# Four raw retention gates of each layer computed in the first attention heads; the first queries' waits and three weight splits placed differently

## The reference, cut to what matters

```python
(rq, rk, rv, rg, cq, ckv, kr, gq, gk, gv, gates) = jnp.split(p, split_at, axis=-1)   # p = h @ w_in
# retention, 4 heads of 128 (q, k) and 256 (v): decayed scores, then the readout
y = rms_norm(y).reshape(B, T, RET_W)
return (jax.nn.silu(g.astype(jnp.float32)) * y).astype(g.dtype)                      # g = rg
# latent attention, 8 heads; grouped-query attention, 8 query heads on 2 key heads
p = softmax(q @ k.T * scale); y = p @ v
# merge
z = sigmoid(gates0) * (y_ret @ w_ret_o) + sigmoid(gates1) * (y_mla @ w_mla_o) + sigmoid(gates2) * (y_gqa @ w_gqa_o)
x = x + mod2 * (z @ w_out)
```

## Time and profile before

| what | value |
|---|---|
| median of three runs | 3587.95 us (3586.75 to 3588.75) |
| profiled execution | 3589.15 us, span in the trace 3587.4 us |
| mean granted TensorE clock | 0.958 of full |
| PE busy / PEld / DVE / ACT / POOL | 3253.7 / 2750.4 / 1517.0 / 1256.1 / 397.5 us |
| chain that ended last | PE 45%, issue 7%, DVE 5%, ACT 2%, DMA 1%, POOL 1% of the span |
| DMA | 309.76 MB, mean 86 GB/s |

### The profile page before, as it was taken

The page is one execution under the profiler, slowest core; times in us unless marked ns, Lnnn a source line. Parts: engine busy times, 40 slices in busy tenths (PEclk is TensorE's granted clock), DMA queues, the critical chain, the costliest instruction groups (busy, mean ns, idle before and its releaser), DMA issues.

```text
span 3587.4 us, 50087 instructions
## 1 busy us (share of the span) xinstructions
PE 3253.7 (91%) x18776; PEld 2750.4 (77%) x18776; DVE 1517.0 (42%) x2025; ACT 1256.1 (35%) x1769; POOL 397.5 (11%) x304
## 2 busy tenths in 40 slices
PE   6799997999898988899999978998799898889998
PEld 5688876888787777788888857787677776768886
DVE  4555423445335433422222355553455455443334
ACT  3344432445323332221211233443255444432222
POOL 0011100111102101010100101110011101011001
PEclk9899998999999999999999988998899899989999
DMA  4122141111331133123132422222121232232222
GB/s 178 56 71 75 69 127 37 59 53 59 107 107 54 60 117 128 49 83 128 59 132 79 138 103 74 69 85 77 54 71 64 71 116 69 85 105 94 99 94 99
DMA packets 98094, 309.76 MB, mean 86 GB/s; under 512 B 10832, under 2 KB 20176, under 8 KB 98000
## 3 DMA queue, kind: packets, MB, share of 16 engines
q1 hardware_dynamic: 55872, 202.40, 16.8%
q10 hardware_dynamic: 42128, 106.07, 8.8%
HBM read 281.17 MB, written 27.26 MB: 86 GB/s over the span
## 4 chain that ended last, share of the span: by engine, by line
PE 45%; issue 7%; DVE 5%; ACT 2%; DMA 1%; POOL 1%; ACTq 0%; DVEq 0%; POOLq 0%
PE ps L1334 43%; PE ps L1437 1%; DVE mx L875 1%; PE ps L1415 1%; POOL ptl L1316 1%; ACT wh L399 1%; DVE tmp L854 1%; DVE wl L844 0%; DVE ptl L893 0%; DMA mraw<-in_wmod 0%; DVE tmp L914 0%; ACT pth L452 0%; ACT side L475 0%; PE ps L1451 0%; DVE hl L1053 0%
## 5 line engine op out<-in xcount | busy, mean ns | idle before, releaser
L1334 PE MATMUL ps<-hh,wh 128*128 128x512 f32 x2768 | 826.9, 359 | 84.6 <-DVE wl L844 33.2
L1334 PE MATMUL ps<-hl,wh 128*128 128x512 f32 x2768 | 815.2, 355 | 0.0
L1334 PE MATMUL ps<-hh,wl 128*128 128x512 f32 x2768 | 815.1, 355 | 0.0
L844 DVE TENSOR_TENSOR wl<-raw,wh 128x1024 fp32r<-128x1024 f32 x364 | 484.7, 1332 | 683.8 <-ACT wh L399 657.1
L1334 PEld LDWEIGHTS ps<-hh,wh 128*128 128x128 f32 x2768 | 456.7, 192 | 173.8 <-issue 46.8
L1334 PEld LDWEIGHTS ps<-hl,wh 128*128 128x128 f32 x2768 | 456.5, 192 | 73.9
L1334 PEld LDWEIGHTS ps<-hh,wl 128*128 128x128 f32 x2768 | 454.9, 191 | 75.4
L399 ACT ACTIVATE wh<-raw 128x1024 fp32r<-128x1024 f32 x364 | 382.4, 1051 | 246.4 <-PE ps L1334 204.9
L1334 PE MATMUL ps<-yh,wh 128*128 128x512 f32 (+1 forms) x1296 | 410.7, 371 | 37.9 <-DVE yl L1185 17.1
L1334 PE MATMUL ps<-yl,wh 128*128 128x512 f32 (+1 forms) x1296 | 398.0, 362 | 0.0
L1334 PE MATMUL ps<-yh,wl 128*128 128x512 f32 (+1 forms) x1296 | 397.6, 361 | 0.0
(11 more groups left out here) (185 smaller groups left out, 3471.7 us busy)
## 6 DMA issues: line engine op xcount, KB each, us to landing
raw<-in_stream SPq DMA_DIRECT2D x364, 512.0 KB, 3.3
mraw<-in_wmod ACTq DMA_DIRECT2D x40, 512.0 KB, 3.3
prob<-in_wmod ACTq DMA_DIRECT2D x40, 512.0 KB, 3.3
gspill<-prob ACTq DMA_DIRECT2D x32, 384.0 KB, 2.3
tmp<-gspill ACTq DMA_DIRECT2D x24, 384.0 KB, 3.1
early<-in_wmod SPq DMA_DIRECT2D x16, 512.0 KB, 15.1
vraw<-gspill ACTq DMA_DIRECT2D x16, 384.0 KB, 3.6
dec<-in_dec ACTq DMA_DIRECT2D x8, 768.0 KB, 4.3
```

Of the source, the lines that this page charges most:

```text
L844: dve.tensor_tensor(wl[:, s, :], raw[:, s, :], wh[:, s, :].bitcast(F32), ALU.subtract).then_inc(sem("w_lo"), 1)
L1334: ins = pe.matmul(out, lhs[w], rhs[x](cols), start=start and n == 0, stop=stop and n == 2)
```

## The change

**Plan.** Of each retention head's two gates the second (column tile 2h+1) is no longer projected in `ret`. The four of a layer are projected in the first heads, two in `mla_first` (heads 0 and 1) and two in `gqa_first` (heads 2 and 3), with 768 columns in layer 0 and 512 in layer 1. The weight chunks move with them in the stream. The results are spilled to a new DRAM tensor `gheld` and read back in `ret`.

**First heads.** The held gates use the slots 1 and 0 in this order, between the first query's projection and the rest of the first head. TensorE's wait ahead of the first query is now for the query ranks alone (`mla_first`) or for the last `vl` (`gqa_first`); in `mla_first` a wait for all ranks stands before the key's projection.

**Splits.** In `mla_in` split 5 stands before the second square root and reciprocal. In `gqa_in` split 3 stands after the first square root on ACT and after the first reciprocal on DVE. In `ret` a head has three chunks: split 4 stands after the one gate's Silu on ACT, is left out in the last head, and split 5 is gone.

**`ret`.** Two heads a loop turn (`half_turn`). ACT issues the DMA of the held gate after the key's rotation, takes its Silu in place after split 4, and then goes on to the `pth` copies. TensorE waits for the two slots after the first two scores instead of before them.

```diff
+HELD = {"chunk": 2, "free0": 1, "free1": 1, "g_out": 2}
-        phase("mla_first", layer, 0, {}, total(head, head, *raws, attention(nq, first=1)), nt=nt)
+        phase("mla_first", layer, 0, {}, total(head, head, HELD, *raws, attention(nq, first=1)), nt=nt)
...
+def half_turn(ph, i, h):
+    return At(dict(ph, base=add(ph["base"], ph["head"], h)), i)
...
+    if alone:                                    # gqa_steps
+        return (0, 1)[:nq // 2 - 1], ((1,), (3,))
...
@@ ACT, spill
-            def spill(at, kc, f, kg, nt, full):
+            def spill(at, kc, f, kg, nt, full, held_at, skip):
+                slot = 1 if held_at is not None and kg == 0 else 0
...
+                row = spilled(at.v("g_row", kg - skip)) if held_at is None else held(held_at)
...
-                act.activation(stage, value, ACT.Copy).then_inc(sem("free0"), 1)
-                act.wait_ge(sem("free0"), at.v("free0", f + 1))
+                act.activation(stage, value, ACT.Copy).then_inc(sem(f"free{slot}"), 1)
+                act.wait_ge(sem(f"free{slot}"), at.v(f"free{slot}", f + 1))
                 act.dma_start(row, stage).then_inc(sem("g_out"), 16)
@@ ACT, mla_in (DVE likewise, before rstd)
+                        if j:
+                            split(at, 5)
                         std(at, j, nt_j, MLA_RANK)
...
-                    split(at, 5)
                     split(at, 6)
@@ ACT and DVE, first heads
-                    c1, f1 = (2, 3) if kind == "mla_first" else (1, 1)
-                    fill = head(at, 0, 0, 0, 0, 0, raws=0)
+                    c1, f1, h0 = (4, 4, 0) if kind == "mla_first" else (3, 2, 2)
+                    fill = head(at, 0, 0, 0, 0, 0, held_at=RET_HEADS * layer + h0)
@@ ACT, gqa_in (DVE likewise, after rstd)
-                        split(at, 2 * j + 1)
+                        if j == 0:
+                            split(at, 1)
...
                         std(at, j, TOK, GQA_HD)
+                        if j == 0:
+                            split(at, 3)
@@ ACT, ret
-                        for e in range(2):
-                            act.wait_ge(sem("product"), t.v("chunk", 3 + e))
-                            if e == 0:
-                                act.wait_ge(sem("v_lo"), t.v("v_lo", 2))
-                            act.activation(tmp[:, 1 + e, 0:nt], pair(e)[:, 0:nt], ACT.Silu).then_inc(
-                                sem(f"free{e}"), 1)
-                            if e == 0:
-                                split(t, 4)
+                        act.dma_start(tmp[:, 2, 0:nt], held(2 * i + (RET_HEADS * layer + h))[:, 0:nt]).then_inc(
+                            sem("rg_in"), 16)
+                        act.wait_ge(sem("product"), t.v("chunk", 3))
+                        act.activation(tmp[:, 1, 0:nt], pair(0)[:, 0:nt], ACT.Silu).then_inc(sem("free0"), 1)
+                        if not last:
+                            split(t, 4)
+                        act.wait_ge(sem("rg_in"), t.v("rg_in", 1) * 16)
+                        act.activation(tmp[:, 2, 0:nt], tmp[:, 2, 0:nt], ACT.Silu)
...
-                        if not last:
-                            split(t, 5)
                         act.wait_ge(sem("v_stat"), t.v("v_stat", 1))
@@ PE, first heads (gate() takes a slot; head 0's key waits for its ranks)
-                    pe.wait_ge(sem("v_lo"), at.v("v_lo"))
-                    fill = head(at, 0, 0, 0, raws=0)
+                    if kind == "gqa_first":
+                        pe.wait_ge(sem("vt_lo"), at.v("vt_lo"))
+                    else:
+                        pe.wait_ge(sem("v_lo"), at.v("v_lo", -4))
+                    fill = head(at, 0, 0, 0, alone=True)
...
+                        if alone:
+                            pe.wait_ge(sem("v_lo"), at.v("v_lo", -2))
@@ PE, ret
-                        for e in range(2):
-                            project(t, 2 + e, e, 1, H, KT, nt, whole)
+                        project(t, 2, 0, 1, H, KT, nt, whole)
                         pe.wait_ge(sem("v_lo"), t.v("v_lo", 2))
-                        for e in range(2):
-                            pe.wait_ge(sem(f"free{e}"), t.v(f"free{e}", 2))
...
                         score(0)
                         score(1)
+                        for e in range(2):
+                            pe.wait_ge(sem(f"free{e}"), t.v(f"free{e}", 2 - e))
@@ stream_of
+        def held_gates(h):
+            for r in (h, h + 1):
+                put(col(O_RG, 2 * r + 1))
...
-            for e in range(2):
-                put(col(O_RG, 2 * h + e))
+            put(col(O_RG, 2 * h))
```

More of the change, by code:

```diff
@@ L158, in plan @@
         raws = [SPILLED] * GQA_RAWS
-        phase("gqa_first", layer, 0, {}, total(query, query, *raws, attention(nq, first=1)), nt=nt)
+        phase("gqa_first", layer, 0, {}, total(query, query, HELD, *raws, attention(nq, first=1)), nt=nt)
         phase("gqa", layer, GQA_HEADS // 2 - 1, total(query, query, att, att, *raws, *raws), nt=nt)
@@ L467, in spill @@
                     act.wait_ge(sem("g_out"), out * 16)
+                row = spilled(at.v("g_row", kg - skip)) if held_at is None else held(held_at)
                 if full:
-                    stage, row, value = prob[:, 3, 0:nt], spilled(out), pair(0)[:, 0:nt]
+                    stage, row, value = prob[:, 3, 0:nt], row[:, 0:nt], pair(slot)[:, 0:nt]
                 else:
@@ L506, in mla_head, with gqa_query @@
                 return fill
-            def gqa_query(at, c0, f0, kq, kg, par, nt, layer, raws=GQA_RAWS, query=True):
+            def gqa_query(at, c0, f0, kq, kg, par, nt, layer, raws=GQA_RAWS, query=True, held_at=None, skip=0):
                 col = layer * G_LAYER + 2 * KT + 2 * RKT
-                qs, pieces = gqa_steps(nt // P, raws)
+                qs, pieces = gqa_steps(nt // P, raws, held_at is not None)
                 def fill(n):
@@ L533, in fill @@
                         if n == steps[-1]:
-                            spill(at, c0 + query + j, f0 + query + j, kg + j, nt, nt > LAT)
+                            spill(at, c0 + query + j, f0 + query + j if held_at is None else j, kg + j,
+                                  nt, nt > LAT,
+                                  None if held_at is None else held_at + j, skip)
                 return fill
@@ L926, in query_lo, with mla_head @@
                     sem("v_lo"), 1)
-            def mla_head(at, c0, f0, kp, kg, par, nt, raws=MLA_RAWS, query=True):
+            def mla_head(at, c0, f0, kp, kg, par, nt, raws=MLA_RAWS, query=True, alone=False):
                 q, pieces, k, v = mla_steps(nt // P, raws)
@@ L1145, in _, with turn @@
                     split(at, 1)
-                    def turn(i, last=False):
-                        t = At(ph, i)
+                    def turn(i, h, last=False):
+                        t = half_turn(ph, i, h)
                         split(t, 2)
@@ L1470, in fill @@
                     for j, steps in enumerate(pieces):
-                        gate(at, c0 + query + j, f0 + query + j, steps, n, (nt, TOK)[j])
+                        gate(at, c0 + query + j, j if alone else f0 + query + j, steps, n, widths[j],
+                             1 - j if alone else 0)
                     if query and n == k:
+                        if alone:
+                            pe.wait_ge(sem("v_lo"), at.v("v_lo", -2))
                         pe.wait_ge(sem("free0"), at.v("free0", fk))
@@ L1490, in mla_head, with gqa_query @@
                 return fill
-            def gqa_query(at, c0, f0, kq, nt, raws=GQA_RAWS, query=True):
-                qs, pieces = gqa_steps(nt // P, raws)
+            def gqa_query(at, c0, f0, kq, nt, raws=GQA_RAWS, query=True, alone=False):
+                qs, pieces = gqa_steps(nt // P, raws, alone)
                 def fill(n):
@@ L1505, in fill @@
                     for j, steps in enumerate(pieces):
-                        gate(at, c0 + query + j, f0 + query + j, steps, n, nt)
+                        gate(at, c0 + query + j, j if alone else f0 + query + j, steps, n, nt, 1 - j if alone else 0)
                 return fill
@@ L1623, in _, with turn @@
                     pe.wait_ge(sem("m_add"), at.v("m_add"))
-                    with pe.Fori(0, turns) as i:
-                        t = At(ph, i)
+                    def turn(t):
                         project(t, 0, 0, 0, H, KT, nt, whole)
@@ L1674, in _ @@
                         ins.then_inc(sem("v_stat"), 1)
+                    with pe.Fori(0, turns) as i:
+                        for h in range(2):
+                            turn(half_turn(ph, i, h))
                 elif kind == "out":
```

101 lines of the change are left out of this document (60 added, 41 removed).

## The result

The kernel after takes 3564.07 us (median of four, 3558.77 to 3569.77) against 3588.35 (3586.75 to 3590.85): ratio 0.9933, 95% interval 0.9921 to 0.9945. The forecast was 3558, range 3540 to 3577. The profiled execution of after is the shortest of its four, 3558.77 against 3589.15: 30.4 us less, where the ledger has 29.8. The sum is right; several terms and the story around them are not: the two first latent heads came out 13.0 us worse than forecast and retention 14.6 better, and that these cancel is luck.

What follows compares the result with a forecast made beforehand. TensorE bounds the kernel (matmuls cover 91% of the span), so only its idle or slow-clock time pays. First heads -12.4, retention -17.4 and 0 sum to -29.8; 3589.15 - 29.8 - 1.2 = 3558 us, range 3540 to 3577.

Steps and rivals of the forecast that it cites:

- Split 5, first query, first gate's start: Latent input, layer 0: projection 5 runs 100.4 to 104.6, the query starts at 107.2, the first held gate at 114.0.
- First latent head: Start of attention moves by +2.0 us in layer 0 and -4.5 in layer 1, with two held gates moved in.
- values 4.1: First latent head: value matmuls take 4.1 us at full clock, against 6.99 at a clock of 0.58 in before.
- First grouped head: Earlier split 3 and query, with two gates moved in: -3.3 us in layer 0, -6.6 in layer 1.
- Retention, layer 0: One projection fewer a head: -25.4 us over four heads, plus 8.0 for lost clock, net -17.4.
- Retention, layer 1: Vector chain leads: 7.9 us gained over four heads, 8.0 lost to the clock, net 0.
- The cited rule: Retention loop: an idle stretch in every turn drops the clock to half in every turn; 2.0 us a head charged.
- (a): Retention heads: the clock holds; 16 us better, 3542; chance 0.16.
- (b): Retention heads: clock down longer, 3.5 us a head instead of 2.0; 12 worse, up to 3574; chance 0.16.
- (c): First heads: queries do not start early, something needed comes with k2l; 1.2 and 4.7 a layer, 3570; chance 0.05.
- (d): Retention: ACT waits for the gate's DRAM read before the pth copies; at 9 us 41 worse, 3599; chance 0.05.
- (e): First heads: gates not hidden, half of their 45 us stays on the path; 22 to 25 worse, about 3582; chance 0.05.

Runs made afterwards that it cites:

- e3: Kernel after with retention's split 4 and the held gate's Silu moved behind the third decay unit: 3547.43 us, ratio 0.9884 to before.
- a0: The kernel after again, unchanged, on the chip of e1, e3 and e4: 3566.85 us, ratio 0.9937 to before.
- e2: Kernel after with the old wait for the last key's low part (k2l) put back before the first query: 3575.50 us, ratio 0.9961 to before.
- e1: Kernel before with only the input stages' splits moved (5 latent, 3 grouped): 3560.49 us, ratio 0.9924.
- e5: Kernel after with split 5 (latent) and split 3 (grouped) back at their old places: 3594.03 us, ratio 1.0002 to before.
- e8: Kernel before with e1's moved splits and early first queries, no held gates, retention unchanged: 3539.15 us, ratio 0.9862.
- e4: Kernel before with only the retention loop written two heads a turn: 3592.13 us, ratio 1.0007.
- e7: e3 with the first held gate's split moved earlier and the grouped query no longer waiting for vl: 3527.58 us, ratio 0.9816 to before.
- f1: e7 without the two held gates of layer 1's latent head, retention heads written out without a loop: 3520.73 us, ratio 0.9800 to before.
- f2: e7 without the held gates of both latent heads, retention heads written out without a loop: 3523.62 us, ratio 0.9816 to before.
- a7: e7 again, unchanged, beside f1 and f2: 3530.84 us, ratio 0.9830 to before.

## Why the prediction was right, step by step

- **Split 5, first query, first gate's start:** right to 0.3 us. **First latent head:** +2.0 forecast, +7.0 measured in layer 0, -4.5 and +3.5 in layer 1. The failed term is the values: "values 4.1", and the 1.0 of half clock that attention was to be spared. I took the gates in front of them as a warm run; the values nevertheless ran at 0.57, and the half clock, granted from 139.2, lasted into attention. Why it fell there, behind 19 us of matmuls, a pause of 0.95, the key and a wait of 1.88, no run separates. That is 2.8 (attention starts 6.9 behind the first value matmul, not 4.1) and 1.0 of the 5.0 missed; the rest is mostly gates of 19.0 instead of 18.4 and 0.35 in the spill copy and the key. In layer 1 the same term is the largest: 7.5 from the first value matmul to attention (2152.79 to 2160.27) instead of 4.1, which is 3.4 of the 8.0 missed; its gates took 13.55 instead of 12.7, and the rest is not traced here. The idle before the query and the gates came as forecast.
- **First grouped head:** -3.3 forecast and -3.2 measured; layer 1 -6.6 and -7.5. Taken from the shift of 6.6 before it (7.0 - 0.4), query and scores come at 590.1 and 618.3 against 590.3 and 618.7.
- **Retention, layer 0:** forecast 5.8 less 2.0 a head, measured 4.5 in the first head and 5.8 in the next two (58.40 - 52.63), and -24.6 over the stage instead of -17.4. The mis-sized term is the wait on `ptl`: 3.53, not 4.5. I let the Silu's table load stand where it stood behind `kl` in the old order; it now follows `kh` at once (1119.19), beside `kl`. The other is the clock: 1.4 by the arithmetic under e3, in a head at 0.97, not 2.0; 2.6 in the first head at 0.94 (53.86 against the 51.24 of a0's third). The last head, charged 2.0 too, waits 1.87 and has no dip there at all.
- **Retention, layer 1:** 0 forecast, -7.4 measured in after, -3.4 in a0. The dip comes every turn as forecast, but in after its place was wrong: it falls on the scores, which have 1.99 us of wait behind them. TensorE in the second head, scores and wait, then the rest; first after, then a0:

```profile
2947.74:2953.40 5.66, 3.67 (x9) 0.70 0.29 90
2953.40:2992.40 39.00, 33.57 (x158) 1.00 0.23 75
```

```profile
2948.89:2954.55 5.66, 3.29 (x10) 0.60 0.26 85
2954.55:2996.16 41.61, 36.20 (x158) 0.93 0.22 72
```

  In after the 9 score matmuls are slowed, the first value matmul still comes when `ptl` is there, and the other 39 us are at 1.00. The head lasts 44.66 instead of 47.07 (2975.35 to 3022.42 of before). I charged 2.0 of clock for it; the half clock under that wait cost nothing. But a0 is the same kernel, and there the dip outlasted the wait: the rest of the head takes 41.61 at 0.93, 2.6 more, and the second and third heads last 47.27 and 47.37, no less than before. So the 2.0 was not wrong as a price; how far the dip reaches changes from execution to execution, and my ledger had one value for it.
- **The cited rule,** a drop in every turn of a loop with an idle stretch (the Trainium skill, TensorE: Matmul & The Clock Gate, "HAM oscillation — how this bites in real kernels"): the traces agree in most turns. After shows it in three of four heads of layer 0 and in all of layer 1, and e3 shows it gone in layer 0's second head when the wait falls from 3.53 to 1.51. It is not every turn, though: a0's third head waited 3.54 and kept 1.00, and e3's first waited 1.84 and dropped (0.97). The rule was worth its place in the sum; the size has to come from what the half clock lies on.
- **Rivals.** (a) The clock did not hold in after (0.94, 0.97, 0.97), but e3 shows what holding it brings. (b) Did not come in after; its longer dip shows in layer 1 of a0. (c) Fell: the queries start early; without that (e2) it is 8.7 worse, 12 were forecast. (d) Fell: ACT issues the read at 1118.34 and its Silu starts at 1122.14, right behind `wh`; no wait. (e) Is half true. The gates' split did come late by 3.98 in the latent head, as charged. (Its 45 us is too low by the ledger's own prices, which give 55.7; half of that would be 28 worse, about 3586.) But I priced the gates against idle time that two other edits of the same change remove, and no part of my ledger asks what those would give without the gates. e1, e5 and e8 show it: the moved splits alone bring 27 (by the ratio), with early queries 50, and the gates as placed take 27 back.
- **What I did not forecast:** +6.1 between retention and layer 1, where nothing changed. It is most likely no effect of the change (below): e4, which has no gate moved, shows +6.6 there. The profiled execution of after lies 5.3 under its median, that of before 0.8 over; of the gap between ledger and medians that is the whole.

## What to carry to other kernels

Price each edit against the kernel that has the others, not against the one before: filling idle time and removing its cause are two claims on the same microseconds. Put a split that only a later projection needs behind the units that start the next chain (e3: 19 us for a move of a few lines), and the one that the idle engine waits for ahead of the long chain (e1: 27 to 30 us). Work held over for a hole needs its operands ready before the hole, and pays only where what it frees is on the path: 9.3 us a head where TensorE leads, 2.9 to 4.2 where the vector chain does. And price a fall of the clock by the work it lies on: 1.4 us on dense matmuls, nothing where a wait follows that takes it up.

## What the hardware showed that I had not expected

At a granted clock of 1.00, with TensorE busy without a gap, the same feed-forward code runs at two paces, in different executions of the same kernel. TensorE in two stretches of 60 us, at the same distance behind retention (340 to 460 us): before, after, and after again.

```profile
1701.50:1761.50 60.00, 60.00 (x348) 1.00 0.18 59
1761.50:1821.50 60.00, 60.00 (x348) 1.00 0.20 69
```

```profile
1676.82:1736.82 60.00, 60.00 (x342) 1.00 0.18 61
1736.82:1796.82 60.00, 60.00 (x341) 1.00 0.20 67
```

```profile
1679.41:1739.41 60.00, 60.00 (x348) 1.00 0.18 60
1739.41:1799.41 60.00, 60.00 (x348) 1.00 0.20 69
```

348 against 341 matmuls is 2%. Single lines show it too: six pairs from 1761.61 to 1763.69 in before (2.08 us) and from 1737.12 to 1739.24 in after (2.12). The granted clock does not tell the two apart; between after and a0 the kernel is the same, and the DMA share too. Counted in four such stretches, 160, 340, 400 and 580 us behind retention, the slow pace (339 or 340 matmuls, against 346 or 347) fell on all four in e7, on three in after, on two in e4, e5, f1 and f2, on one in a0, e3 and a7, and on none in before, e1, e2 and e8. The feed-forward stage follows it: +8.1; +6.1; +6.6, +6.7, +4.2, +4.4; +3.4, +2.3, +2.5; 0, -0.8, +2.0, -3.3. So the pace accounts for most of what that stage shows, and it may be part of the spread of 8 to 19 us between runs of one kernel. What sets it stays open.
